# Attention: values for four query tiles at a time, the squares and the eps term summed by one product, heads written out

## What is computed

```python
    def attend(q_blk):
        s = jnp.einsum('bqhcd,bkhcd->bhcqk', q_blk, k, preferred_element_type=jnp.float32)
        p = jax.nn.softmax(s, axis=-1)
        a = p[:, :, 0] - lam * p[:, :, 1]
        return jnp.einsum('bhqk,bkhe->bqhe', a.astype(v.dtype), v)
...
    o = rms_norm(o, subln_g) * (1.0 - lambda_init)
    return o.reshape(B, S, N_HEADS * V_DIM) @ w_o
```

## Time and profile before

| what | value |
|---|---|
| time, median of 3 runs | 2425.22 us (2424.23 to 2425.43) |
| time of the profiled execution | 2422.12 us |
| its span, first to last instruction | 2420.3 us |
| mean granted TensorE clock | 0.993 |
| PE busy, share of the span | 2350.3 us, 97% |
| PE weight loads | 1947.1 us, 80% |
| DVE busy | 1357.0 us, 56% |
| POOL busy | 1050.0 us, 43% |
| ACT busy | 949.7 us, 39% |

### The profile page before, as it was taken

One profiled execution on the slowest core, in us unless ns is written; L12 is line 12 of the kernel. 1 busy time (PEld: TensorE's weight loads), 2 busy tenths in 40 slices (PEclk: granted clock), 3 DMA queues, 4 the chain that ended last, 5 costly groups with the idle time before them and its releaser, 6 DMA issues.

```text
span 2420.3 us, 28034 instructions
## 1 busy us (share of the span) xinstructions
PE 2350.3 (97%) x10948; PEld 1947.1 (80%) x10948; DVE 1357.0 (56%) x1240; ACT 949.7 (39%) x1149; POOL 1050.0 (43%) x725
## 2 busy tenths in 40 slices
PE   8899989999999999999999999999999999999997
PEld 6688778888877888888888888888878888888886
DVE  7566799999475555556422233344655555564223
ACT  5111278888444444444311321113454444442112
POOL 1112134444367677775122422213687666742221
PEclk9899999999999999999999999999999999999998
DMA  3453373432222222222522111112222222234222
GB/s 129 165 173 122 131 214 101 120 98 76 86 83 84 87 79 79 87 88 99 197 90 81 56 44 49 47 52 87 96 70 93 81 87 79 79 131 174 90 79 93
DMA packets 73799, 239.45 MB, mean 99 GB/s; under 512 B 8160, under 2 KB 8544, under 8 KB 73696
## 3 DMA queue, kind: packets, MB, share of 16 engines
q1 hardware_dynamic: 73696, 238.01, 29.9%
HBM read 177.16 MB, written 60.82 MB: 98 GB/s over the span
## 4 chain that ended last, share of the span: by engine, by line
PE 76%; issue 13%; ACT 4%; DVE 3%; POOL 3%; DMA 0%; POOLq 0%; DVEq 0%; ACTq 0%
PE PS L282 35%; PE PS L766 11%; PE PS L767 11%; PE PS L768 11%; PE PS L679 2%; DVE nb L1281 2%; POOL Wst L267 2%; PE PS L656 1%; PE PS L657 1%; PE PS L664 1%; ACT X L962 1%; ACT X L974 1%; ACT sq L974 1%; POOL X L1621 1%; PE PS L690 1%
## 5 line engine op out<-in xcount | busy, mean ns | idle before, releaser
L267 POOL TENSOR_TENSOR Wst<-Wraw,Wst 128x1024 fp32r<-128x1024 f32 (+1 forms) x111 | 263.0, 2371 | 877.5 <-ACT Wst L261 877.5
L766 PE MATMUL PS<-XB,U 128*128 128x512 f32 x1208 | 471.1, 390 | 6.9 <-POOL U L1615 6.8
L768 PE MATMUL PS<-XB,U 128*128 128x512 f32 x1224 | 476.7, 389 | 0.0
L282 PE MATMUL PS<-H,Wst 128*128 128x512 f32 x2070 | 470.1, 389 | 0.6 <-issue 0.3
L767 PE MATMUL PS<-XB,U 128*128 128x512 f32 x1208 | 470.4, 389 | 0.0
L282 PEld LDWEIGHTS PS<-H,Wst 128*128 128x128 f32 x2070 | 388.4, 188 | 81.9 <-issue 1.3
L282 PE MATMUL PS<-XGh,Wst 128*128 128x512 f32 x1536 | 420.3, 394 | 25.5 <-POOL Wst L267 13.0
L261 ACT ACTIVATE Wst<-Wraw 128x1024 fp32r<-128x1024 f32 (+1 forms) x111 | 113.9, 1028 | 652.3 <-DMA Wraw<-weights 652.2
L282 PEld LDWEIGHTS PS<-XGh,Wst 128*128 128x128 f32 x1536 | 290.1, 190 | 89.2 <-issue 24.6
L766 PEld LDWEIGHTS PS<-XB,U 128*128 128x128 f32 x1208 | 227.1, 188 | 55.9 <-POOL U L1615 7.6
L768 PEld LDWEIGHTS PS<-XB,U 128*128 128x128 f32 x1224 | 230.0, 188 | 48.0
(11 more groups left out here) (191 smaller groups left out, 3311.2 us busy)
## 6 DMA issues: line engine op xcount, KB each, us to landing
Wraw<-weights SPq DMA_DIRECT2D x79, 512.0 KB, 3.5
U1f<-ups SPq DMA_DIRECT2D x44, 512.0 KB, 4.6
U2f<-ups SPq DMA_DIRECT2D x44, 512.0 KB, 3.8
h_scratch<-Tv SPq DMA_DIRECT2D x44, 512.0 KB, 5.4
Hf<-h_scratch SPq DMA_DIRECT2D x44, 512.0 KB, 4.7
Wraw<-weights SPq DMA_DIRECT2D x32, 448.0 KB, 3.2
x_scratch<-X SPq DMA_DIRECT2D x16, 512.0 KB, 3.1
X<-x_scratch SPq DMA_DIRECT2D x16, 512.0 KB, 7.1
```

The costliest lines, as they stand in the source:

```text
L267: pool.tensor_tensor(w[:, 1, 0:cols], raw[:, 0:cols], w[:, 0, 0:cols].bitcast(F32), ALU.subtract).then_inc(w_lo, 1)
L282: ins = pe.matmul(ps[:, h * HALF:(h + 1) * HALF], w, m[:, h * HALF:(h + 1) * HALF], start=begin, stop=last and w is wl)
L766: pe.matmul(ps, wh, bh, start=begin, stop=False, skip_group_check=True)
L768: ins = pe.matmul(ps, wl, bh, start=False, stop=kp == KP - 1, skip_group_check=True)
```

## The change

- Values of four query tiles at a time: the products of `values` have 512 columns instead of 256, and there are half as many. A group of four tiles (u = 2h or 2h+1) gets them in three parts: key tiles 0 to 2 (9 products) in the step that is six behind the group's first tile, 3 to 6 (12 products) in the next, and 7 (3 products) in the one after, there ahead of the transposes. No values in the fourth step.
- The transposed probabilities lie in pairs of tiles, three buffers for the high and three for the low parts; the second pair of each group goes to the same buffer for every group. ScalarE therefore waits for `pv_done` of the group before, ahead of the third tile of a group.
- The eps term: GpSimd adds the diagonal tiles `dg` to the squares `osq` (one addition of 512 columns for four tiles), and `subln_sum` is one float32 product of 512 columns. GpSimd makes each `dg` five steps later than before, from row sums kept in `s0sq`.
- The square, the scaled copy, the logarithm, the exponential, the norm's product and the high and low parts of its result have 512 columns and come once in four steps: square and scaled copy, and the high part of the group before, in the step with i a multiple of 4; low part and addition of `dg` in the next; `subln_sum`, logarithm and exponential in the one after; the norm's product in the fourth.
- All eight heads are written out on PE, DVE, ACT and POOL; the loop is gone. The tail is two steps longer, and `dense_ahead` skips its third and fourth step. A staging buffer for one weight tile of w_o and some small tiles lie elsewhere; the DMAs are the same.

```diff
-        Ah = [XGl[:, 2 * b:2 * b + 2, :].rearrange("p a (t n) -> p (a t) n", n=2 * P) for b in range(2)]
-        Al = [XGl[:, 4 + 2 * b:6 + 2 * b, :].rearrange("p a (t n) -> p (a t) n", n=2 * P) for b in range(2)]
-        osq, osb, z, ot = (sq[:, 0, t * 2 * P:(t + 1) * 2 * P] for t in range(4))
-        ot3 = sq[:, 0:1, 6 * P:8 * P]
-        dg = cu[:, 0:QT * P]
...
+        At = at("At", [P, 17, 2 * S], AR + 32 * K, F32R)
+        A_HI, A_LO = ((1, 16), (2, 16)), ((0, 4), (3, 4))
+        on_q = at("on_q", [P, 4, HALF], AR + 148 * K)
+        osq, osb, z, ot = (on_q[:, t, :] for t in range(4))
+        dg = at("dg", [P, HALF], ER + 16 * K)
+        def a_tile(where, q):
+            block = where[q // 4][q // 2 % 2]
+            return At[:, block, :].rearrange("p (t n) -> p t n", n=2 * P)[:, :, q % 2 * P:(q % 2 + 1) * P]
...
-        def run_steps(eng, step, last):
-            for ii in range(QT):
-                step(0, ii, first=True, parity=0)
-            with eng.Fori(0, HEADS // 2 - 1) as pair:
-                for a in range(2):
-                    for ii in range(QT):
-                        step(pair * 2 + (1 + a), ii, parity=1 - a)
-            for ii in range(QT):
-                step(HEADS - 1, ii, parity=1)
+        def lagged(h, q, tail):
+            return h * QT + q >= 0 and (not tail or q < QT)
...
+        def run_steps(step, last):
+            for h in range(HEADS):
+                for ii in range(QT):
+                    step(h, ii)
             for ii in range(QT, last + 1):
-                step(HEADS - 1, ii, tail=True, parity=1)
+                step(HEADS - 1, ii, tail=True)
...
-                for t in range(4 * part, 4 * part + 4):
+                for t in (range(0, 3), range(3, 7), range(7, 8))[part]:
                     c = slice(t * P, (t + 1) * P)
-                    for w, m in ((0, Ah[b]), (0, Al[b]), (1, Ah[b])):
...
-                        ins = pe.matmul(slot(3)[:, 0:2 * P], VV[parity][w][:, c], m[:, t, :], start=first, stop=last)
-                ins.then_inc((pv_half, pv_done)[part], 1)
-
-            def subln_sum(u, quarter):
-
-                pe.wait_ge(o_sq, u + 1)
-                pe.wait_ge(dg_done, 2 * u + 2)
+                    for w, m in ((0, A_HI), (0, A_LO), (1, A_HI)):
+                        first, last = t == 0 and w == 0 and m is A_HI, t == KT - 1 and w == 1
+                        ins = pe.matmul(slot(3)[:, 0:HALF], VV[parity][w][:, c], a_group(m, g, t),
+                                        start=first, stop=last)
+                if part == 2:
+                    ins.then_inc(pv_done, 1)
+            def subln_sum(u):
+                pe.wait_ge(sqd_done, u + 1)
                 wait(pe, ln_done, u)
-                pe.matmul(slot(3)[:, HALF:HALF + 2 * P], ones[:, :], osq, start=True, stop=False)
-                for t in range(2):
-                    b = 2 * quarter + t
-                    ins = pe.matmul(slot(3)[:, HALF + t * P:HALF + (t + 1) * P], ones[:, :],
-                                    dg[:, b * P:(b + 1) * P], start=False, stop=t == 1)
-                ins.then_inc(ss_done, 1)
+                pe.matmul(slot(3)[:, HALF:S], ones[:, :], osq, start=True, stop=True).then_inc(ss_done, 1)
+            ahead = {0: (0, (0, 1)), 1: (0, (2, 3)), 4: (0, (4, 5, 6)), 5: (1, (0, 1, 2)), 6: (1, (3, 4, 5, 6))}
...
+                def values_of(lag, part):
+                    q = ii - lag
+                    values(h + q // QT, h * 2 + q // 4, q // 4 % 2, part, (h + q // QT) % 2)
+                if on(h, ii - 8, tail):
+                    values_of(8, 2)
+                if lagged(h, ii - 2, tail):
                     transposes(i - 2, (ii - 2) % QT)
-                if on(ii - 6, first, tail):
-                    subln_sum(h * 4 + (ii - 6) // 2, (ii - 6) // 2 % 4)
-                if on(ii - 4, first, tail):
-                    values(h, h * 4 + (ii - 4) // 2, (ii - 4) // 2 % 4, 0, parity if ii >= 4 else 1 - parity)
-                if on(ii - 5, first, tail):
-                    values(h, h * 4 + (ii - 5) // 2, (ii - 5) // 2 % 4, 1, parity if ii >= 5 else 1 - parity)
-                if tail:
-                    dense_ahead(*((0, (0, 1)), (0, (2, 3)), (0, (4, 5, 6)), (1, (0, 1, 2)), (1, (3, 4, 5, 6)))[ii - QT])
+                if on(h, ii - 10, tail):
+                    subln_sum(h * 2 + (ii - 10) // 4)
+                if on(h, ii - 6, tail):
+                    values_of(6, 0)
+                if on(h, ii - 7, tail):
+                    values_of(7, 1)
+                if tail and ii - QT in ahead:
...
-                    if q % 2 == 0:
-                        wait(act, pv_done, h * 4 + (ii - 2) // 2 - 1)
-                    act.activation(Ah[q // 2 % 2][:, :, q % 2 * P:(q % 2 + 1) * P],
-                                   slot(2).rearrange("p (t n) -> p t n", n=P), ACT.Copy).then_inc(ah_made, 1)
+                    if q % 4 == 0:
+                        wait(act, pv_done, h * 2 + (ii - 2) // 4 - 1)
+                    if q % 4 == 2:
+                        wait(act, pv_done, h * 2 + (ii - 2) // 4)
+                    act.activation(a_tile(A_HI, q), slot(2).rearrange("p (t n) -> p t n", n=P), ACT.Copy
...
-                if on(ii - 6, first, tail):
-
-                    u = h * 4 + (ii - 6) // 2
+                if on(h, ii - 10, tail):
+                    u = h * 2 + (ii - 10) // 4
                     act.wait_ge(ss_done, u + 1)
-                    act.activation(z, slot(3)[:, HALF:HALF + 2 * P], ACT.Ln, scale=1.0 / VD).then_inc(ln_done, 1)
+                    wait(act, o_scaled, u)
+                    act.activation(z, slot(3)[:, HALF:S], ACT.Ln, scale=1.0 / VD).then_inc(ln_done, 1)
                     act.wait_ge(ln_done, u + 1)
                     act.activation(z, z, ACT.Exp, scale=-0.5).then_inc(z_done, 1)
-                if on(ii - 5, first, tail):
-                    u = h * 4 + (ii - 5) // 2
+                if on(h, ii - 8, tail):
+                    u = h * 2 + (ii - 8) // 4
                     act.wait_ge(pv_done, u + 1)
+                    wait(act, ss_done, u)
+                    act.activation(osq, slot(3)[:, 0:HALF], ACT.Square).then_inc(o_sq, 1)
                     wait(act, o_scaled, u)
-                    act.activation(osb, slot(3)[:, 0:2 * P], ACT.Copy, scale=lam[:, 5:6]).then_inc(o_copied, 1)
-                    wait(act, ss_done, u)
-                    act.activation(osq, slot(3)[:, 0:2 * P], ACT.Square).then_inc(o_sq, 1)
-                if on(ii - 8, first, tail):
-                    u, uq = h * 4 + (ii - 8) // 2, (ii - 8) // 2
+                    act.activation(osb, slot(3)[:, 0:HALF], ACT.Copy, scale=lam[:, 5:6]).then_inc(o_copied, 1)
+                if on(h, ii - 12, tail):
+                    u = h * 2 + (ii - 12) // 4
                     act.wait_ge(o_scaled, u + 1)
-                    act.activation(Yh[:, bass.ds(h + uq // 4, 1), uq % 4 * 2 * P:(uq % 4 + 1) * 2 * P], ot3, ACT.Copy
+                    act.activation(Yh[:, u // 2, u % 2 * HALF:(u % 2 + 1) * HALF], ot, ACT.Copy
                                    ).then_inc(yh_made, 1)
...
+                if on(h, ii - 13, tail):
+                    u = h * 2 + (ii - 13) // 4
+                    cols = slice(u % 2 * HALF, (u % 2 + 1) * HALF)
                     pool.wait_ge(yh_made, u + 1)
-                    pool.tensor_tensor(Yl[:, dst[0], dst[1]], ot3, Yh[:, dst[0], dst[1]].bitcast(F32), ALU.subtract
+                    pool.tensor_tensor(Yl[:, u // 2, cols], ot, Yh[:, u // 2, cols].bitcast(F32), ALU.subtract
                                        ).then_inc(yl_made, 1)
-                if on(ii - 7, first, tail):
-                    u = h * 4 + (ii - 7) // 2
+                if lagged(h, ii - 6, tail):
+                    q = (ii - 6) % QT
+                    pool.wait_ge(s0sq_done, i - 5)
+                    if q % 4 == 0:
+                        wait(pool, sqd_done, h * 2 + (ii - 6) // 4)
+                    pool.tensor_tensor(dg[:, q % 4 * P:(q % 4 + 1) * P], con[:, C_EPSI:C_EPSI + P],
+                                       s0sq[:, q:q + 1].to_broadcast([P, P]), ALU.mult).then_inc(dg_done, 1)
+                if on(h, ii - 9, tail):
+                    u = h * 2 + (ii - 9) // 4
+                    pool.wait_ge(dg_done, 4 * u + 4)
+                    pool.wait_ge(o_sq, u + 1)
+                    pool.tensor_tensor(osq, osq, dg[:, :], ALU.add).then_inc(sqd_done, 1)
+                if on(h, ii - 11, tail):
+                    u = h * 2 + (ii - 11) // 4
                     pool.wait_ge(z_done, u + 1)
+                    pool.wait_ge(o_copied, u + 1)
                     wait(pool, yl_made, u)
                     pool.tensor_tensor(ot, osb, z, ALU.mult).then_inc(o_scaled, 1)
 
-            run_steps(pool, step, 15)
+            run_steps(step, 17)
```

More of the change, by code:

```diff
@@ L104, in build @@
         coef = sb("coef", [P, 4])
+        s0sq = sb("s0sq", [P, QT])
         epsb = sb("epsb", [P, 1])
```

(19 more changed lines are left out.)

66 lines of the change are left out of this document (29 added, 37 removed).

## The result

| | before | after |
|---|---|---|
| time, median of 5 runs each, measured together | 2425.22 us (2422.83 to 2426.08) | 2438.76 us (2434.1 to 2440.05) |
| ratio after to before | | 1.0056, interval 1.0041 to 1.0070 |
| profiled execution | 2422.12 us | 2438.42 us |
| its span | 2420.3 us | 2436.6 us |
| mean granted TensorE clock | 0.993 | 0.993 |

The account below looks back on a forecast made before the run. Each attention step was taken to cost the larger of VectorE's and PE's shares. PE's heavy steps 12.4, tail -0.95 and GpSimd's stop 2.3 gave +13.8 us on 2425.22: 2439.0 us, range 2427 to 2451.

Parts of the forecast that it names:

- PE's heavy steps, +12.4: Attention loop: values and squares gathered in two steps of four make PE late; four steps 20.63 against 19.72, +12.4 us.
- The step of 12 products: Attention step after the one with squares: 12 products of values on PE, predicted at 5.48 us.
- The squares' step: Attention step where PE sums squares, then does 9 products of values: predicted 5.20 + 0.63 = 5.83 us.
- Light steps: Third and fourth of four attention steps: VectorE's pace of 4.66 us was to hold.
- Rivals 1 and 2: Attention: PE's burst absorbed, 2408.5 us, 12%; or half absorbed, 2425 us or close by, 8%.
- ScalarE at nothing: Third attention step: square, scaled copy and high part take 1.55 us, just hidden in 1.57; taken as 0.
- The low part's stop, +2.3: GpSimd's low part starts ahead of VectorE's combination, delaying PE's transposes 0.18 us for each of 13 groups: +2.3 us.
- GpSimd as the bound (rival 3): Attention: GpSimd's low part, dg and addition, stopped twice, make PE's sum 0.8 late in 14 groups: +11, 2450 us, 10%.
- Tail, -0.95: Attention's tail: less PE work for values and sums, -1.1, with 3 products in front costing +0.15: -0.95 us.
- Heads written out, at nothing: Attention loop: its turns cost nothing, so writing out the heads saves nothing.
- The width, 0.24 us less PE in four steps: PE's values: 24 products of 512 columns take 5.52 us for 5.76, 0.24 less in four steps.
- The sum by one product: PE's squares: one float32 product of 512 columns, 0.86 us, once in four steps, 0.86 less PE work.

Follow-up runs that it names:

- experiment 1: The changed kernel with GpSimd's low part (put behind dg) and norm's product both waiting for VectorE's combination: 2435.14 us, ratio 1.0037.
- experiment 7: The changed kernel with one GpSimd operation waiting for VectorE's combination: only the norm's product, 2433.61 us; only the low part, 2438.94 us.
- the repeat: The kernel before with only the loop over heads written out, measured a second time: 2425.09 us, ratio 1.0003.
- experiment 4: The changed kernel with each 512-column product of values made as two of 256: 2439.42 us.
- experiment 6: The kernel before with GpSimd adding dg to the squares of a pair and the sum made by one 256-column product: 2412.88 us, ratio 0.9946.
- experiment 3: The changed kernel with values of two products instead of three (less exact) and GpSimd's low part and norm's product waiting for VectorE's combination: 2409.96 us.
- experiments 2, 5 and 7: 2: changed kernel, values of two products instead of three, 2429.2 us; 5: kernel before, heads written out, 2422.86 us; 7: see experiment 7.

## Why the prediction was right, and where not

The forecast was 2439.0 us and the time is 2438.76, on the side and inside the range that were given. Part of that nearness is luck. The attention and its tail together were predicted at +13.8 and came to +14.8 (15.25 less 0.43). PE's part of it was predicted at 12.4 - 0.95 = 11.45 and is 11.7 in experiment 1, which has no stops (13.1, less 1.4 in the tail). The other 3.1 us are a stop that the prediction doesn't have, and the stop that it has, at 2.3, cost nothing. And the unchanged code moved by a few us.

- **PE's heavy steps, +12.4: right.** Without the stops (experiment 1) the length is 13.1 us above before. The step of 12 products took 5.43 for 5.48. The squares' step took 5.95 for 5.83. Its path on PE, from the gate to the minimum, was predicted at 5.34 + 0.63 = 5.97 and measured at 5.96. The gate is what differs, 0.03 us ahead of the step's minimum and not 0.14. Light steps stayed at 4.65, as said. Rivals 1 and 2 (the burst absorbed or half absorbed) fall with this.
- **ScalarE at nothing: nearly.** The square, scaled copy and high part run in the kernel after from 490.68 to the next exponential's start at 492.25, 0.05 behind the end of its minimum (490.99 + 1.21): 1.57 us, the 1.55 in a room of 1.57. (Its own rows give 1.26 + 3.22 = 4.48 for the end of the second exponential and not 4.35; but the next operation starts before that end, 4.34 behind the minimum here.) The lateness came from elsewhere: in experiment 1 the copy of the transposes in the light step starts at 491.14, behind transposes of 490.07 + 1.03, where the kernel after has no such wait (488.69, right behind the read at 488.59). That is 0.1 us, which the full room passes on to the gate: the exponential starts at 494.72, its minimum has ended at 494.56. The prediction had the transposes end 2.3 us behind the step's minimum and the copy wanted at 2.4; they ended at 2.42 (488.68 to 491.10).
- **The low part's stop, +2.3: the mechanism right, the size not.** The stop came in the predicted step, with the predicted row: combination 1.95 us, its end 0.7 late. The Trainium skill ("SBUF — State Buffer", section "Who interferes with whom") has the rule that whoever starts first keeps the shared interface for a whole instruction. The trace agrees: VectorE takes 1.28 us when it is first and 1.95 or 2.33 when GpSimd is. But the step that fell was "it adds 0.18 for each of 13 groups". PE's transposes began 1.04 us behind its gate (496.58), as in experiment 1 (498.00 and 499.04), so PE lost nothing: VectorE's late low part ended at 496.39, 0.19 ahead of them. What the low part's step lost, the squares' step, bound by PE, gave back. Measured: 0.0 to 0.1 (experiment 7).
- **The product's stop: missing.** The prediction had looked at the low part alone for a start ahead of the combination. Now that `dg` is made from row sums of an older tile it waits for nothing: it starts 0.15 us behind the small product ahead of it (503.29 and 503.44), where it was 0.27 before (487.80 and 488.07). So it lets the norm's product go at 503.79. The combination follows VectorE's second minimum and starts at 503.84. These 0.05 us make the step 5.71 instead of 5.43, of which the squares' step gives back 0.10 (5.30 to 5.20): 3.1 us in all, 1.0 of it in the tail. That VectorE would wait for nothing but scores in the heavy steps was wrong here.
- **GpSimd as the bound (rival 3): not so.** The addition of `dg` starts at 495.60, and the sum at 497.45 follows the transposes at once. But the side from which it was argued, a second operation of GpSimd beside a combination, is the one that cost.
- **Tail, -0.95: -0.43.** The product's stop is in it too: in experiment 7, which is without it, the tail takes 34.90 us, 1.4 less than before. In the timeline of the kernel after the transposes of the last tile but one wait for VectorE:

```profile
629.15 2.34 DVE L1312 SCALAR_TENSOR_TENSOR R<-R,coef,X 128x1024 f32<-128x1024 f32 x1
...
632.77 1.06 PE L670 MATMUL PS<-con,R 128*128 128x128 f32 x8 [0.79 <-DVE At L1317]
```

  The 1.70 us idle of the earlier trace rows were to be filled, and 0.79 remain.
- **Heads written out, at nothing: right** (1.0003 in the repeat).
- **The width, 0.24 us less PE in four steps:** 0.12 of it arrives (experiment 4), since only the squares' step is PE's in the kernel after.
- **The sum by one product** is the part of the change that gains. By itself it brings 12.7 us (experiment 6). At four tiles it is one float32 sum of 0.86 us in one step of four, on top of nine products; in pairs it is 0.43 in each slow step, where PE has little over VectorE's pace.

## What to carry over

Where two engines hand work back and forth in a fixed order with two buffers, count each step as the larger of the two engines' shares: work saved over four steps is lost if it is gathered in the steps that are already late. Two costs found in neighbouring steps are not to be added; ask of each what is late once the other is there, and try both away together, since one at a time showed 3 and 9 us here of 24. And list every GpSimd operation with its start relative to each VectorE operation of two SBUF inputs, above all those whose waits the change removes: an edit that frees one operation moves all that are queued behind it.

## What the runs showed of the hardware

- A combination of 1024 columns that GpSimd's operation precedes ends 1.08 us behind GpSimd's end in both forms (494.18 and 495.26; 505.09 and 506.17), so it costs more the later GpSimd starts: 0.67 with GpSimd 0.41 ahead, 1.05 with 0.05 ahead. With VectorE 0.08 ahead, as in the earlier trace rows, it costs VectorE nothing.
- The same holds for a small operation of GpSimd. `dg`, 128 columns and 0.40 us, stops a combination if it starts late enough: in the kernel before it once starts 0.10 us ahead, and the combination takes 1.38 us and ends 1.08 behind it (345.14 and 346.22). Where it is 0.25 ahead, the combination would end later than 1.08 behind it anyway, and takes its usual 1.28. The timelines of GpSimd and VectorE, first in the kernel before, then in experiment 3:

```profile
344.74 0.40 POOL L1558 TENSOR_TENSOR cu<-con,coef 128x128 f32<-128x128 f32 x1 [0.17 <-POOL coef L1554]
344.84 1.38 DVE L1300 SCALAR_TENSOR_TENSOR sq<-sq,coef,X 128x1024 f32<-128x1024 f32 x1
```

```profile
503.91 0.40 POOL L1572 TENSOR_TENSOR dg<-con,s0sq 128x128 f32<-128x128 f32 x1
504.16 1.28 DVE L1312 SCALAR_TENSOR_TENSOR X<-X,coef 128x1024 f32<-128x1024 f32 x1
```

- The granted clock of TensorE fell to 0.50 for some 3 or 7 us at a time, in other places in each execution. Where PE set the pace of a step, or came near it, that step grew by 0.55 to 1.2 us (experiments 2, 5 and 7); that is more than the 0.1 us that one stop was worth.
- Two sets of 10 and 11 runs of the same kernel, on two chips, gave 0.9987 and 1.0003 of before, with intervals that barely meet. An interval within one set doesn't contain what differs between sets.
